# The second block's output projection as three f16 products in a one-core transformer kernel

## What is computed

```python
h = rms_norm(x, norm_mix[l])
proj = h @ w_in[l]
...
o_hgrn = hgrn2_mixer(hq, hf, hi, hg, lb_table[l], hgrn_norm[l])
...
o_moba = merge_heads(moba_attention(mq, mk, mv))
mixed = jnp.concatenate([o_hgrn, o_moba.astype(o_hgrn.dtype)], axis=-1)
x = x + mixed @ w_out[l]
h = rms_norm(x, norm_xattn[l])
...
x = x + cross_attention(h, mem_n, w_xq[l], w_xk[l], w_xv[l], w_xo[l])
```

## Time and profile before

| what | us |
|---|---|
| median of 3 runs (lowest, highest) | 825.14 (821.84, 825.64) |
| the profiled execution | 824.1 |
| its span, from the first to the last instruction | 822.3 |
| TensorE busy | 787.0 (96% of the span) |
| VectorE busy | 548.8 (67%) |
| ScalarE busy | 393.5 (48%) |
| GpSimd busy | 71.4 (9%) |
| mean DMA rate | 156 GB/s |

### The profile page before, as it was taken

How to read it: one execution, slowest core, us unless ns; L and a number is a source line. 1 busy time by engine, 2 the same in 40 slices (tenths; PEclk the granted TensorE clock), 3 DMA queues, 4 the chain that set the end, 5 groups by cost and what they waited for, 6 DMA issues and landing times.

```text
span 822.3 us, 17167 instructions
## 1 busy us (share of the span) xinstructions
PE 787.0 (96%) x7490; PEld 663.3 (81%) x7490; DVE 548.8 (67%) x866; ACT 393.5 (48%) x623; POOL 71.4 (9%) x98
## 2 busy tenths in 40 slices
PE   7999978989899999999999999999999999999996
PEld 6788866768686888888886877588878888888885
DVE  4678856646486899999676787654476476664443
ACT  5458441110415566677564764152554375553333
POOL 1142011202001110111001100000200200000000
PEclk9999997989999999999999999999999999999999
DMA  9971230203028365545774264112647145555001
GB/s 333 393 267 66 103 116 3 105 2 106 2 102 290 121 201 186 189 183 183 282 296 173 104 243 167 47 56 103 264 146 265 44 161 196 198 222 222 29 1 52
DMA packets 66555, 127.93 MB, mean 156 GB/s; under 512 B 3760, under 2 KB 27568, under 8 KB 66352
## 3 DMA queue, kind: packets, MB, share of 16 engines
q1 hardware_dynamic: 65168, 122.92, 41.4%
q0 software_dynamic: 592, 2.69, 0.9%
q10 hardware_dynamic: 720, 1.23, 0.4%
HBM read 125.78 MB, written 1.05 MB: 154 GB/s over the span
## 4 chain that ended last, share of the span: by engine, by line
PE 70%; DVE 16%; ACT 5%; issue 4%; DMA 2%; SPq 1%; POOL 1%; DVEq 0%; POOLq 0%
PE bank L502 21%; PE bank L610 19%; DVE arena L490 8%; PE bank L607 7%; DVE arena L1975 3%; PE bank L2062 3%; DMA ring<-in_w_in_dram 2%; PE bank L1246 2%; ACT arena L481 2%; PE bank L756 2%; PE bank L731 2%; PE bank L1265 1%; PE bank L2256 1%; SPq L447 1%; PE bank L2524 1%
## 5 line engine op out<-in xcount | busy, mean ns | idle before, releaser
L490 DVE SCALAR_TENSOR_TENSOR arena<-ring,arena 128x1024 f16<-128x1024 f32 x194 | 230.1, 1232 | 79.4 <-ACT arena L481 79.0
L502 PE MATMUL bank<-hg,arena 128*128 128x256 f16 x2496 | 275.9, 273 | 0.9 <-DVE arena L490 0.8
L502 PEld LDWEIGHTS bank<-hg,arena 128*128 128x128 f16 x2496 | 242.9, 98 | 33.4 <-issue 3.5
L481 ACT ACTIVATE arena<-ring 128x1024 f16<-128x1024 f32 x194 | 191.9, 1045 | 89.4 <-PE bank L610 51.7
L610 PE MATMUL bank<-arena 128*128 128x256 f16 x1296 | 142.2, 273 | 0.2 <-DVE arena L490 0.2
L610 PEld LDWEIGHTS bank<-arena 128*128 128x128 f16 x1296 | 126.6, 98 | 15.5 <-issue 0.9
L607 PE MATMUL bank<-mix,ring 128*128 128x256 f32 x256 | 55.7, 379 | 1.1 <-ACT arena L1907 1.1
L607 PEld LDWEIGHTS bank<-mix,ring 128*128 128x128 f32 x256 | 48.5, 190 | 8.4 <-issue 1.9
L517 ACT ACTIVATE hg<-h,params 128x256 f16<-128x256 f32 (+1 forms) x40 | 20.0, 499 | 57.3 <-DVE h L2470 43.6
L1975 DVE SCALAR_TENSOR_TENSOR arena<-arena,params 128x256 f32<-128x256 f32 x88 | 36.6, 477 | 0.7 <-ACT arena L2009 0.7
L502 PE MATMUL bank<-xv,arena 128*128 128x256 f16 x288 | 32.1, 273 | 0.0
(11 more groups left out here) (368 smaller groups left out, 965.3 us busy)
## 6 DMA issues: line engine op xcount, KB each, us to landing
ring<-in_w_in_dram SPq DMA_DIRECT2D x12, 2048.0 KB, 9.2
ring<-in_ffn_w_up_dram SPq DMA_DIRECT2D x22, 1024.0 KB, 7.5
ring<-in_w_ff_dram SPq DMA_DIRECT2D x8, 2048.0 KB, 8.8
ring<-in_w_ff_dram SPq DMA_DIRECT2D x16, 1024.0 KB, 6.1
ring<-in_ffn_w_down_dram SPq DMA_DIRECT2D x11, 1024.0 KB, 5.9
ring<-in_w_out_dram SPq DMA_DIRECT2D x8, 1024.0 KB, 6.5
ring<-in_w_xk_dram SPq DMA_DIRECT2D x2, 2048.0 KB, 10.2
ring<-in_w_xv_dram SPq DMA_DIRECT2D x2, 2048.0 KB, 7.9
```

Of the source, the lines that this page charges most:

```text
L481: nc.scalar.activation(quarter(halves_of(chunk)[0], chunk, q), quarter(slot(*chunk), chunk, q), ACT.Copy, scale=W_SCALE).then_inc(*mark("w ...
L490: nc.vector.scalar_tensor_tensor(quarter(halves_of(chunk)[1], chunk, q), quarter(slot(*chunk), chunk, q), W_SCALE, quarter(halves_of(chunk ...
L502: mm = nc.tensor.matmul(out_, weight[a][:, k, cols], src[:, k, b, :], start=(first and i == 0), stop=(last and i == 2), skip_group_check=True)
```

## The change

`w_out_2` joins the projections that are multiplied as three f16 products. It doesn't use the split areas of the others (`SPLIT`), but eight quarters of 1024 words at addresses of their own, `OUT_AT`, which other tiles of this stage leave free one after the other. `out_high` on ACT and `out_low` on DVE write the two halves of a quarter. The four quarters of chunk 1 are written inside `dve_project2` and `act_project2`; those of chunk 0 after `dve_hgrn_end` and around the end of `act_project2`, ahead of the high and low halves of `w_xq_2`.

The mix is split too. `act_moba_out` now writes the f16 high half of tiles 4 to 7, and a new DVE subtraction the low half. `dve_hgrn_end` writes the float value of tiles 0 to 3 in place into `GH`, ACT copies each to f16, and DVE subtracts. A load of the square root's table is written out ahead of the second squares. The ring's chunks are marked as used by the last low quarter, no longer by the last matmul, and the residual is scaled by 1/64.

```diff
+OUT_AT = {1: (2048, 0, 1024, 4096), 0: (5120, 7168, 6144, 9216)}
...
+        def out_quarter(i, q):
+            return split_view(view(OUT_AT[i][q], SLOT // 4))
+
+        def out_high(act, i, qs):
+            for q in qs:
+                act.wait_ge(*at("chunk", CHUNK_NO[("w_out_2", "rows", i)]))
+                nc.scalar.activation(out_quarter(i, q)[:, 0, :], slot("w_out_2", "rows", i)[:, q, :], ACT.Copy,
+                                     scale=W_SCALE).then_inc(*mark("out_weights_high", "out high", i, q))
+
+        def out_low(dve, i, qs):
+            for q in qs:
+                dve.wait_ge(*at("out high", i, q))
+                nc.vector.scalar_tensor_tensor(out_quarter(i, q)[:, 1, :], slot("w_out_2", "rows", i)[:, q, :],
+                                               W_SCALE, out_quarter(i, q)[:, 0, :], ALU.mult,
+                                               ALU.subtract).then_inc(*mark("out_weights_low", "out low", i, q))
+                if q == 3:
+                    chunk_used("w_out_2", "rows", i, ("out low", i, q))
...
                 for n, (a, b) in enumerate(((0, 0), (1, 0), (0, 1))):
-                    mm = nc.tensor.matmul(out_, halves_of((name, "rows", i))[a][:, kk, cols], src[:, k, b, :],
-                                          start=(first and n == 0), stop=(last and n == 2), skip_group_check=True)
+                    weight = halves_of((name, "rows", i))[a][:, kk, cols] if stored else \
+                        out_quarter(i, kk)[:, a, cols]
+                    mm = nc.tensor.matmul(out_, weight, src[:, k, b, :], start=(first and n == 0),
+                                          stop=(last and n == 2), skip_group_check=True)
...
                     pe.wait_ge(*at(*src_ready(4 * i + kk)))
-                    if split:
+                    if stored:
                         pe.wait_ge(*at("low", SPLIT_NO[(name, "rows", i)], kk))
+                    elif split:
+                        pe.wait_ge(*at("out low", i, kk))
...
             dve_moba_normal(dve, (0, 1))
+            out_low(dve, 1, (0,))
             scaled(GH, 0, lambda b: ("hgate bank", b), "hgate scaled", (0,))
             dve_hgrn_sums(dve, 1)
             dve_moba_normal(dve, (2, 3))
             dve_hgrn_unit(dve)
+            out_low(dve, 1, (1,))
             scaled(GH, 0, lambda b: ("hgate bank", b), "hgate scaled", (1,))
+            out_low(dve, 1, (2, 3))
+            for i in range(2):
+                dve.wait_ge(*at("mix2 high", 4 + 2 * i))
+                nc.vector.tensor_tensor(mix16[:, 4 + 2 * i:6 + 2 * i, 1, :], halves(2 + i),
+                                        mix16[:, 4 + 2 * i:6 + 2 * i, 0, :], ALU.subtract).then_inc(
+                    *mark("moba_vector", "mix2", 4 + 2 * i))
+                same(("mix2", 5 + 2 * i), ("mix2", 4 + 2 * i))
             dve_hgrn_end(dve)
+            out_low(dve, 0, range(4))
...
             act_moba(act, (2, 3))
+            act.wait_ge(*at("rotated", 1))
+            out_high(act, 1, (0,))
+            nc.scalar.preload_act_table_set("sqrt_and_others")
             act_hgrn_squares(act, 1)
+            out_high(act, 1, (1, 2))
             act_hgrn_root(act)
             nc.scalar.preload_act_table_set("silu_and_others")
+            out_high(act, 1, (3,))
             act_moba_probabilities(act)
             act.wait_ge(*at("hgate scaled", 1))
             nc.scalar.activation(flat(GH), flat(GH), ACT.Silu).then_inc(*mark("hgrn_act", "hgate"))
             act_moba_out(act)
+            out_high(act, 0, (0,))
+            for j in range(4):
+                act.wait_ge(*at("mix2 float", j))
+                nc.scalar.activation(mix16[:, j, 0, :], GH[:, j, :], ACT.Copy).then_inc(
+                    *mark("hgrn_act", "mix2 high", j))
+            out_high(act, 0, (1, 2, 3))
...
             for j in range(4):
-                nc.vector.scalar_tensor_tensor(mix[:, j, :], halves(j // 2)[:, j % 2, :], par("hgrn_norm_2", j),
+                nc.vector.scalar_tensor_tensor(GH[:, j, :], halves(j // 2)[:, j % 2, :], par("hgrn_norm_2", j),
                                                GH[:, j, :], ALU.mult, ALU.mult).then_inc(
+                    *mark("hgrn_vector", "mix2 float", j))
+            for j in range(4):
+                dve.wait_ge(*at("mix2 high", j))
+                nc.vector.tensor_tensor(mix16[:, j, 1, :], GH[:, j, :], mix16[:, j, 0, :], ALU.subtract).then_inc(
                     *mark("hgrn_vector", "mix2", j))
...
-                nc.scalar.activation(mix[:, 4 + 2 * i:6 + 2 * i, :], halves(2 + i), ACT.Copy).then_inc(
-                    *mark("moba_act", "mix2", 4 + 2 * i))
-                same(("mix2", 5 + 2 * i), ("mix2", 4 + 2 * i))
+                nc.scalar.activation(mix16[:, 4 + 2 * i:6 + 2 * i, 0, :], halves(2 + i), ACT.Copy).then_inc(
+                    *mark("moba_act", "mix2 high", 4 + 2 * i))
...
-            dve_residual(dve, "out2", 1.0, "norm_xattn", "norm_xattn_2")
+            dve_residual(dve, "out2", 1.0 / W_SCALE, "norm_xattn", "norm_xattn_2")
```

More of the change, by code:

```diff
@@ L595, in narrow @@
             order = order or range((ktiles + 3) // 4)
-            split = (name, "rows", 0) in SPLIT_NO
+            stored = (name, "rows", 0) in SPLIT_NO
+            split = stored or name == "w_out_2"
             for b in range(4):
@@ L636, in narrow @@
                             mm.then_inc(*mark("projected_out", label, "bank", m // 2))
-                if split:
+                if stored:
                     split_used((name, "rows", i), used)
-                else:
+                elif not split:
                     chunk_used(name, "rows", i, used)
@@ L2730, in _ @@
             pe_project2(pe)
-            narrow(pe, "w_out_2", KT, mix, lambda k: ("mix2", k), "out2",
+            narrow(pe, "w_out_2", KT, mix16, lambda k: ("mix2", k), "out2",
                    lambda b: ("moba p", b) if b < 2 else ("o unit", b - 2), order=(1, 0))
```

## The result

The changed kernel takes 818.0 us (median of 5 runs, 816.06 to 819.09), the one before 825.14 us. The two medians lie 7.1 us apart; the ratio of the runs is 0.9918, with a 95% interval of 0.9893 to 0.9944, which is 6.8 us less. The forecast was 817.9 us and 6.7 us less.

The account below looks back on a forecast made before the run. TensorE, busy 96% of the span, was taken as the bound; 6.7 us less in the output projection, all added work at cost 0, gave 824.6 - 6.7 = 817.9 us. Its own range was 816 to 820, 8 in 10 815.5 to 822.

Parts of the forecast that it names:

- The size: Output projection w_out_2 on TensorE: 27.63 us in f32 falls to the 20.96 us of cross-attention's f16 form, 6.67 us less.
- ScalarE and VectorE, chunk 1: Casts of w_out_2's chunk 1 in the MoBA stage's waits: cost 0, with 1.4 us of slack on ScalarE.
- The walk: The prediction's pass in order through the waits of ScalarE and VectorE, placing 9.4 and 12.5 us of added work beside TensorE.
- Chunk 0 and the mix: Chunk 0's casts and the mix subtractions around the HGRN end: cost 0, slack 5 us on the first low quarter.
- What came last: VectorE reaches the first residual 0.2 us late after w_xq_2's low halves; cost 0, with 1.6 us of slack for TensorE.
- Rival (1): Queues become the bound: w_xq_2's late low halves make TensorE wait before the next projection; 820 to 822 us, chance 0.14.
- Rival (2): MoBA-stage waits don't cover the casts: 11.1 us uncovered against 6.67 gained, 828.5 us, about 4.4 slower; chance 0.05.
- the alternative with a drain: By the Trainium skill's 1380 ns drain per table switch: 2.7 us more before the probabilities, gain about 5.5 us.
- Rival (3): Lower granted clock in the new projection after new waits; 13 us of it would eat the gain (824.6 us); chance 0.05.
- Rival (4): Three f16 matmuls from scattered quarters take TensorE as long as one f32 product; 824.6 us, chance 0.04.
- Ring and DMA: Ring slots come free at 551.4 and 561.6, so w_xo_2's loads start earlier; gain and cost 0.

Follow-up runs that it names:

- two_more_loads: Changed kernel plus two more ScalarE table loads before the probabilities; TensorE's hole at the copies grew from 0.63 to 1.63 us.
- two_products: Changed kernel without the product of low weights and high mix in w_out_2, 64 matmuls less; 816.72 us in one execution.
- four_more: Changed kernel plus four extra low casts (4.6 us) on VectorE ahead of the low halves of w_xq_2; 818.39 us, one run.
- eight_more: Changed kernel plus eight extra low casts (9.2 us) on VectorE ahead of the low halves of w_xq_2; 825.27 us, one run.
- casts_only: Changed kernel with all sixteen w_out_2 casts kept, but the projection multiplied in f32 from an unsplit mix; 823.5 us, ratio 1.0013 to the kernel before.
- no_casts: Changed kernel without the sixteen w_out_2 casts, its f16 products reading constants as weights; 814.86 us, ratio 0.9911 to the kernel before.
- casts_in_a_block: Changed kernel with chunk 1's eight casts moved from the MoBA stage's waits into one block behind it; 821.19 us, ratio 0.9971 to the kernel before.
- four_more_filled: Changed kernel plus four extra VectorE low casts, with 12 constant matmuls filling TensorE's wait behind the projection; 822.1 us in one execution.
- two_products_filled: Changed kernel with only two products in w_out_2, and 22 constant matmuls filling TensorE's wait behind it; 813.7 us in one execution.
- before: The kernel before the change, with w_out_2 multiplied in f32; 825.14 us, its projection 27.63 us.
- late_release: Changed kernel with w_out_2's two ring slots given back by TensorE's last matmul, as before the change; projection still 20.96 us from start to start.

## Why the prediction was right

**The size.** The term that carries the sum, 27.63 - 20.96, was read from a stretch where the same routine already ran in the new form on the same number of products. It came out at 6.67, to the last digit.

**ScalarE and VectorE, chunk 1.** The walk, shifted by the 1.05 us by which this trace is early, is met within 0.1 us: the moved load starts at 539.2 of the old time, the squares at 540.5, the first copies at 546.4, the last ones at 548.7. ScalarE's idle time before the last copies is 1.47 us, and the slack was put at 1.4. `two_more_loads` used it up and paid for the rest: 1.58 us are measured.

**Chunk 0 and the mix.** One price was too high. VectorE's four subtractions of 128x256 took 418 ns each, between the bounds of 0.35 and 0.49 us; I had taken the upper, from an f32 addition. But 489 ns is the mean of a group of 16 whose shortest, median and longest are 410, 416 and 715 ns, and the median would have been the right price. From the first subtraction to the next cast it was 1.34 us, where the walk had 1.6, and `dve_hgrn_end` was 0.1 us shorter than put. So VectorE ended its low quarters at 561.25 of the old time, not at 561.6. The first residual began at 570.5, 17.23 us after the projection's start, which is the moment its bank is ready by the pattern of the earlier trace rows. VectorE's queue would have allowed some 0.13 us earlier: the residual follows the start of the eight low halves by 9.22 us here, and by 9.08 in `two_products`, where the bank had long been ready. So VectorE wasn't 0.2 us late for that bank, as the walk said, but 0.13 us early.

**What came last.** The prediction named VectorE's arrival at the first residual as the next bound, with 1.6 us of slack. `four_more`, `eight_more` and `two_products` give 1.97: the last step of the walk (TensorE 1.9 us behind the first residual) was right, and the 0.37 us more are what VectorE was early by. Rival (1) was thus true as a mechanism and wrong as to the point from which it decides.

**Rival (2)**, casts that aren't covered, fell with `casts_only` and `no_casts`. But the mechanism exists: with chunk 1's casts in a block 3.9 us are given back, 2.26 of them by a later start and 1.67 by the clock. How much the 11.1 us of its bound could come to was not tried. Its time of 828.5 adds the 4.4 us to 824.1 instead of the 824.6 that the forecast starts from; it should be 829.0. (In the alternative with a drain, 2.7 - 1.4 likewise leaves 1.3 us and not 1.2. Neither bears on the forecast.)

**Rival (3)**, the clock: in the changed kernel it stayed at 1.00 through the projection. The condition in the text (new waits ahead of it) was the right one, as `casts_in_a_block` shows, but there the lower clock lasted some 3.4 us and cost 1.67, where the rival needed 13 us of it to eat the gain. **Rival (4)** fell with 20.96 us from scattered quarters. **Ring and DMA**: put at nothing, measured at nothing.

The whole time, 817.9 against 818.0, is closer than the method deserves: the middle of four times of before, which differ by 3.8 us, happened to fit. That part is luck; the 6.67 us is not.

## What to carry to other kernels

Price a new form of a product where the same routine already runs in that form, and then walk the two elementwise queues wait by wait to see whether the preparation fits; here both came out within 0.4 us. Look at the median of a group before its mean is used as a price. Put preparation work into the queues' existing waits, each piece ahead of a wait that is longer than it is. Compare small edits by distances inside the trace, anchored at an instruction just ahead of the edit, when the whole time scatters by more than half of what is sought.

## What the runs showed of the hardware

**A hole in TensorE's work can cost more than its length.** In four runs with a hole of 2.11, 2.52, 4.85 and 7.18 us the matmuls behind it ran at a granted clock of 0.50 for some 3.4 to 5.5 us and lost 1.67, 1.67, 2.66 and 2.66 us on top. With the hole filled by matmuls that serve nothing, the loss was gone in both kernels tried, each traced once. Holes of 0.63 us never did this. Those of 1.7 us before the attention's turned probabilities (in all 14 traces) were followed by a lower clock in three, `two_more_loads`, `four_more_filled` and `two_products_filled`, at a price of 1.45 to 1.64 us; those of 1.72 us before cross-attention's output projection in none of 14. So it isn't the length alone that decides, and what else does stays open.

**TensorE can be busy and lose its clock.** In the kernel before it was at 0.57 from 518 to 522 without any hole; the changed kernel's profiled execution was at 1.00 there:

```profile
518.00:522.00 4.00, 4.00 (x16) 1.00 0.00 0
```

No edit lies ahead of that point. The price can be read over all traces. From the earlier norm's total (at 440.19 in the changed kernel) to the hole at the copies it is 108.4 us in ten of them, with the clock at 1.00 from 517 to 524. In the other four, `before`, `casts_only`, `two_more_loads` (less the 1.0 us of its loads) and `late_release`, it is 110.0 to 110.1 us, with a clock of 0.76 in that window: 1.65 us for each such fall. The hole at the copies as a whole came between 546.2 and 551.3 us. The rest of that spread lies ahead of 440 us, where windows of lower clock between 117 and 193 us differ from run to run; I take them for its source, though no run isolates it.

**An f32 matmul** of 128x256 shows as two records and takes 432 ns, so three f16 matmuls at 109 ns each are cheaper by a quarter. **A subtraction in SBUF** with an f16 operand and result took 415 to 421 ns for 128x256. That is what an f32 addition of that size usually takes (median 416 ns in the kernel before), so the f16 operand gained nothing there.
